# One product on 8 partitions for the relative-bias tables, rows repeated by the DMA; top-k's second tile turned three units later

## What is computed

```python
sc = jnp.einsum('bshpc,hpkc->bshpk', q, sub_keys).astype(jnp.float32)
top_v, top_i = lax.top_k(sc, PEER_TOPK)
...
best_v, best_pos = lax.top_k(cand_v, PEER_TOPK)
idx = jnp.take_along_axis(cand_i, best_pos, axis=-1)
gate = jax.nn.softmax(best_v, axis=-1)
```

```python
dist = qi - kj
in_win = (dist >= 0) & (dist < SWA_WINDOW)
bias = rel_bias.astype(jnp.float32)[t5_bucket(jnp.maximum(dist, 0))]
...
s = jnp.where(valid[None, :, None, None], s + bias[None, None], -jnp.inf)
```

## Time and profile before

| | |
|---|---|
| median of 3 runs | 2253.37 us (2249.6 to 2253.55) |
| the profiled execution | 2255.65 us |
| its span | 2254.1 us |
| TensorE busy (PE) | 2179.7 us, 97% |
| DVE, ScalarE (ACT), GpSimd (POOL) busy | 1362.5, 1228.5, 918.5 us |
| mean DMA rate | 165 GB/s |

### The profile page before, as it was taken

The page is one execution under the profiler, slowest core; times in us unless marked ns, Lnnn a source line. Parts: engine busy times, 40 slices in busy tenths (PEclk is TensorE's granted clock), DMA queues, the critical chain, the costliest instruction groups (busy, mean ns, idle before and its releaser), DMA issues.

```text
span 2254.1 us, 38404 instructions
## 1 busy us (share of the span) xinstructions
PE 2179.7 (97%) x15186; PEld 2037.3 (90%) x15186; DVE 1362.5 (60%) x2552; ACT 1228.5 (55%) x2201; POOL 918.5 (41%) x429
## 2 busy tenths in 40 slices
PE   8999899999999999999999998999999999899999
PEld 7988889999999998888888898999998899799997
DVE  3557652998666756666665765356654764546664
ACT  5657544455777765455453555645445355555443
POOL 4664436898666640000006674450002666361000
PEclk9999999999999999999999999999999999999999
DMA  6544455665444456666664554455665445355664
GB/s 211 157 125 121 148 161 178 181 186 167 141 141 141 148 182 194 195 192 193 195 179 155 190 164 126 123 183 155 184 189 174 150 141 162 109 161 167 182 184 158
DMA packets 104085, 371.70 MB, mean 165 GB/s; under 512 B 11490, under 2 KB 13922, under 8 KB 103268
## 3 DMA queue, kind: packets, MB, share of 16 engines
q1 hardware_dynamic: 103908, 369.25, 53.7%
HBM read 365.53 MB, written 3.67 MB: 164 GB/s over the span
## 4 chain that ended last, share of the span: by engine, by line
PE 78%; DVE 13%; ACT 5%; issue 2%; DMA 1%; POOL 1%; SPq 0%; DVEq 0%; ACTq 0%; POOLq 0%
PE stream_bank L558 13%; PE stream_bank L560 13%; PE stream_bank L559 13%; PE side_bank L560 10%; PE side_bank L558 10%; PE side_bank L559 10%; PE side_bank L811 1%; ACT unit_hi L1071 1%; PE side_bank L810 1%; PE side_bank L620 1%; DVE hot L1942 1%; ACT squares L1097 1%; PE side_bank L639 1%; DVE hot L1945 1%; POOL unit_lo L2326 1%
## 5 line engine op out<-in xcount | busy, mean ns | idle before, releaser
L2326 POOL TENSOR_TENSOR unit_lo<-raw,unit_hi 128x1024 fp32r<-128x1024 f32 (+1 forms) x362 | 880.0, 2436 | 500.3 <-ACT unit_hi L1071 499.0
L1071 ACT ACTIVATE unit_hi<-raw 128x1024 fp32r<-128x1024 f32 (+1 forms) x678 | 708.3, 1045 | 212.5 <-PE side_bank L560 91.4
L1601 DVE TENSOR_TENSOR unit_lo<-raw,unit_hi 128x1024 fp32r<-128x1024 f32 (+1 forms) x316 | 386.4, 1223 | 275.9 <-ACT unit_hi L1071 275.4
L558 PE MATMUL stream_bank<-hT_hi,unit_hi 128*128 128x256 f32 x1672 | 493.3, 295 | 1.0 <-POOL unit_lo L2326 1.0
L559 PE MATMUL stream_bank<-hT_lo,unit_hi 128*128 128x256 f32 x1672 | 477.3, 285 | 0.0
L560 PE MATMUL stream_bank<-hT_hi,unit_lo 128*128 128x256 f32 x1672 | 477.2, 285 | 0.0
L558 PEld LDWEIGHTS stream_bank<-hT_hi,unit_hi 128*128 128x128 f32 x1672 | 325.1, 194 | 9.9 <-issue 6.3
L558 PE MATMUL stream_bank<-h2T_hi,unit_hi 128*128 128x256 f32 x1152 | 330.8, 287 | 0.0
L560 PE MATMUL stream_bank<-h2T_hi,unit_lo 128*128 128x256 f32 x1152 | 327.0, 284 | 0.0
L559 PE MATMUL stream_bank<-h2T_lo,unit_hi 128*128 128x256 f32 x1152 | 326.9, 284 | 0.0
L559 PEld LDWEIGHTS stream_bank<-hT_lo,unit_hi 128*128 128x128 f32 x1672 | 324.9, 194 | 1.6
(11 more groups left out here) (343 smaller groups left out, 4128.5 us busy)
## 6 DMA issues: line engine op xcount, KB each, us to landing
raw<-in_peer_u_dram SPq DMA_DIRECT2D x128, 512.0 KB, 3.6
raw<-in_peer_v_dram SPq DMA_DIRECT2D x128, 512.0 KB, 3.6
raw<-in_gate_dram SPq DMA_DIRECT2D x64, 512.0 KB, 3.6
raw<-in_gt_dram SPq DMA_DIRECT2D x44, 512.0 KB, 3.6
raw<-in_up_dram SPq DMA_DIRECT2D x44, 512.0 KB, 3.6
raw<-in_ffn_out_dram SPq DMA_DIRECT2D x44, 512.0 KB, 3.6
raw<-in_branch_dram SPq DMA_DIRECT2D x32, 512.0 KB, 3.7
raw<-in_w_gate_dram SPq DMA_DIRECT2D x24, 512.0 KB, 3.6
```

The lines of the kernel that those rows point to most:

```text
L558: mm(out, l.hi, r.hi, start=start, stop=False)
L1071: activation(k.unit_hi[n % SPLIT_SLOTS][:, 0:w], k.raw[n % RAW_SLOTS][:, 0:w], ACT.Copy).then_inc(k.sem("unit_hi"), 1)
L1601: V.tensor_tensor(k.unit_lo[s][:, 0:w], k.raw[n % RAW_SLOTS][:, 0:w], k.unit_hi[s][:, 0:w], ALU.subtract).then_inc(unit_lo, 1)
L2326: G.tensor_tensor(k.unit_lo[s][:, 0:w], k.raw[n % RAW_SLOTS][:, 0:w], k.unit_hi[s][:, 0:w], ALU.subtract).then_inc(k.sem("unit_lo_pool"), 1)
```

## The change

Two groups of edits. The second tile's turn goes from behind unit 54 to behind unit 57, its exponential from 46 to 49, the groups of gates start at unit 58 and are spread over 67. And the bias rows are made by one product with the 8 heads on 8 partitions, one addition on 8 partitions; SP writes them 128 times over, by a source that repeats each partition's row with a step of 0, behind the layer's load 11; the wait for the landing and the eight fetches begin at load 16.

```diff
-GATES_FROM, GATES_OVER = 55, 70
-SLOTS_EXP, SLOTS_TURN = (21, 46), (28, 54)
+GATES_FROM, GATES_OVER = 58, 67
+SLOTS_EXP, SLOTS_TURN = (21, 49), (28, 57)
...
-        self.rel_wide = self.place("rel_bias_wide", [P, SWA_HEADS, P], at=at + 8 * SKEW + 32)
-        self.bias_rows = self.place("bias_rows", [P, SWA_HEADS, SKEW], at=at + 8 * SKEW + 32 + 4096)
+        self.bias_rows = self.place("bias_rows", [P, SKEW], at=at + 8 * SKEW + 32)
...
-            for h in range(SWA_HEADS):
-                bank = take(SIDE + 2 + h % 2, ("bias", h))
-                if h == 0:
-                    pe.wait_ge(k.sem("landed_bias_consts"), 32)
-                    pe.wait_ge(k.sem("rel_wide"), 1)
-                mm(bank[:, 0:SKEW], k.rel_wide[0:BUCKETS, h, :], k.bias_consts[0:BUCKETS, 0:SKEW],
-                   start=True, stop=True).then_inc(k.sem("bias_mm"), 1)
-                yield
-            for h in range(SWA_HEADS):
+            bank = take(SIDE + 2, ("bias",))
+            pe.wait_ge(k.sem("landed_bias_consts"), 32)
+            mm(bank[0:SWA_HEADS, 0:SKEW], k.rel_bias[0:BUCKETS, :], k.bias_consts[0:BUCKETS, 0:SKEW],
+               start=True, stop=True).then_inc(k.sem("bias_mm"), 1)
+            yield
+            for _ in range(SWA_HEADS):
                 yield
...
-            for _ in range(5 + 2 * SWA_HEADS):
+            for _ in range(6 + SWA_HEADS):
                 yield
             act.wait_ge(k.sem("landed_bias_rows"), 16)
...
-            dve.wait_ge(k.sem("landed_bias_consts"), 32)
-            V.tensor_copy(k.rel_wide[0:BUCKETS, :, :], wide(k.rel_bias[0:BUCKETS, :], P)).then_inc(k.sem("rel_wide"), 1)
+            dve.wait_ge(k.sem("bias_mm"), 1)
+            V.tensor_tensor(k.bias_rows[0:SWA_HEADS, :], k.bank[SIDE + 2][0:SWA_HEADS, 0:SKEW],
+                            k.bias_consts[0:SWA_HEADS, SKEW:], ALU.add).then_inc(k.free[SIDE + 2], 1)
             yield
...
-    load_until(U["cg.0", 0] + 19)
+    load_until(U["cg.0", 0] + 12)
     scratch = nc.dram_tensor("bias_scratch", [SWA_HEADS * P * SKEW], F32, kind="Internal").ap()
-    sp.wait_ge(*k.over["bias", SWA_HEADS - 2])
-    sp.wait_ge(*k.over["bias", SWA_HEADS - 1])
-    fetch(scratch.rearrange("(h p m) -> p h m", h=SWA_HEADS, p=P), k.bias_rows[:, :, :], "landed_bias_rows")
+    sp.wait_ge(*k.over[("bias",)])
+    rows = k.bias_rows[0:SWA_HEADS, :].unsqueeze(1).to_broadcast([SWA_HEADS, P, SKEW])
+    fetch(scratch.rearrange("(h p m) -> h p m", h=SWA_HEADS, p=P), rows, "landed_bias_rows")
     for h in range(SWA_HEADS):
-        load_until(U["cg.0", 0] + 19 + h)
+        load_until(U["cg.0", 0] + 16 + h)
         if h == 0:
             sp.wait_ge(k.sem("landed_bias_rows"), 16)
```

More of the change, by code:

```diff
@@ L2041, in bias_tables @@
         def bias_tables():
-            for _ in range(4):
+            for _ in range(5):
                 yield
-            dve.wait_ge(k.sem("landed_bias_consts"), 32)
-            V.tensor_copy(k.rel_wide[0:BUCKETS, :, :], wide(k.rel_bias[0:BUCKETS, :], P)).then_inc(k.sem("rel_wide"), 1)
+            dve.wait_ge(k.sem("bias_mm"), 1)
+            V.tensor_tensor(k.bias_rows[0:SWA_HEADS, :], k.bank[SIDE + 2][0:SWA_HEADS, 0:SKEW],
+                            k.bias_consts[0:SWA_HEADS, SKEW:], ALU.add).then_inc(k.free[SIDE + 2], 1)
             yield
[L2047 to L2053, removed]
+            for _ in range(SWA_HEADS):
                 yield
```

## The result

| | us |
|---|---|
| before, median of 4 runs | 2253.46 (2249.6 to 2253.71) |
| after, median of 4 runs | 2267.59 (2263.54 to 2270.52) |
| ratio | 1.0063, 95% interval 1.005 to 1.0076 |
| after, the profiled execution; its span | 2268.49; 2267.0 |

The changed kernel is slower by 0.6%, about 14 us.

A forecast was written before the change was run, and what follows sets the result against it. TensorE, busy 97% of the span, was taken as the bound. Terms -8.2 - 6.9 + 14.8 + 2.6, with 0.2 for the lo half, gave +2.5: 2255.9 us on the median, 8-in-10 range 2236 to 2262.

The forecast's parts named there:

- Term 2: Layer's relative-bias rows: one TensorE product in place of eight gains 6.9 us, the five waits on `bias_rows` included.
- Term 3: Bias write to DRAM from 8 partitions takes 31 us to landing, delays layer unit 12's load: stall 14.8 us, low clock 2.6.
- rival A: Bias write lands within 16.2 us and is hidden, so no stall: 2238.5 us; chance 0.35.
- beyond T = 16.2, one for one: T is the bias write's time from issue to landing; TensorE stalls at layer unit 12 by whatever exceeds 16.2 us.
- The low clock behind the stall: After the stall at layer unit 12 TensorE comes back at the low clock, costing 2.6 us.
- Term 1: Top-k's second turn, unit 54 to 57: gains 8.2 us (5.4 stall, 2.4 low clock, 0.4 turn at low clock).
- rival C: POOL and DVE collide differently, `picked` ends over 3.2 us later, TensorE stalls at unit 57: 2246.5 us; chance 0.02 with write hidden.
- rival B: Same write stall with T over 33 us: 2261.9 us at two engines' worth, 2296.9 at one; chance 0.26.

The follow-up runs named there:

- the 128-partition kernel: Changed kernel with each head's bias column repeated 16 times, so one product fills 128 partitions and the write repeats each row 8 times: 2242.85 us, ratio 0.9959.
- The three narrow widths: Bias rows written from 8 partitions (the changed kernel), 16 or 32 adjacent partitions, otherwise as in the change: 2267.59, 2254.39 and 2242.88 us.
- the 17-us write: Changed kernel with bias rows on 16 partitions, 2254.39 us; with ScalarE evicting units 9 and 10 before unit 12's hi half, 2249.51 us.

## Why the prediction was wrong

**Term 2, one product for eight, -6.9: right.** Six products fewer in the stretch gave 5.95 in the 128-partition kernel (5.9 forecast), the changed kernel's trace has one product left, of 0.81, and no wait on `bias_rows`. With 128 partitions and the turn the kernel is 9.2 us faster, 2.5 of it the turn: 6.7.

**Term 3, the write's time, 31: right, within 1.5 us.** 32.5 by itself, and 34.0 to unit 12's hi half with the load's 1.45 behind it. As far as the rows go this was luck: 31 was the middle of two bounds, three and two engines' worth, and no row set either. The estimate by the Trainium skill's port table, which had 31.1, gave a reason for it and was borne out, and rival A, a write hidden by its cover, fell.

**Term 3, where the stall begins: the step that failed.** I wrote: "Unit 12 began at 1233.72; six of the seven products taken out lie before it, so it now wants to begin at 1233.72 - 5.9 = 1227.8", and from that "beyond T = 16.2, one for one". The data are wanted then, but they are waited for earlier. Every engine that prepares the stream waits for a load three units before TensorE uses it, and has other work queued behind that wait: ScalarE the eviction of unit 9, GpSimd the rotary multiply of unit 9. The stall began at 1214.4, ahead of unit 10, and was 23.3 us where 14.8 was forecast: by the forecast's own rule a write of 32.5 gives 16.3, and the start of the stall two units sooner makes up the rest. The three narrow widths show the true point at 9.1 to 9.8 us, and changing the order alone took 5 us of stall away from the 17-us write. I had even asked, of SP's and ScalarE's wait for `landed_bias_rows`, what stands behind them; I did not ask it of the wait for the delayed load. The low clock behind the stall, 2.6 forecast, came to about 1.9: of the 23.3 the rotary product waits 0.6 in any case, and 24.6 less 22.7 is left. The whole term: 24.6 in place of 17.4.

**Term 1, the turn, -8.2: mis-sized.** Every row behind it was read rightly, and the mechanism is as told, but the 5.4 us of stall and the 2.4 of low clock were one execution's: the step that failed here is taking the price of the turn from one profile. Its time, 2255.65, lay 2.28 above the median, and the forecast only shifted the sum by that. Two further profiles of the same top-k have 3.25 and none, with no low clock. Timed, the term is -2.5 (-0.5 to -4.5). In rows of the changed kernel the turn comes free (no wait on `picked`), and the waits on lo halves are 1.5 us, as in the second profile of before (1.0 in the first), so rival C took no part.

**The sum.** Forecast +2.5; with the two terms as measured, -2.5 - 6.7 + 24.6 = +15.4; measured +14.2. The forecast's rival B, this same mechanism with a longer write, was on the right side but for the wrong reason: it wanted T over 33, where 32.5 was enough with the stall begun ahead of unit 10 and not of unit 12.

## What to carry to other kernels

Ask of a late load not when its data are used, but which instruction first waits for it, on each engine, and what stands behind that instruction; the slack ends there. A write from few adjacent partitions can be slow (32.5 us from 8, 5.7 from 128, for the same bytes), by the ports that they lie behind if the Trainium skill's table (page "SBUF — State Buffer", section "Door 1: The DMA port swizzle") holds as it did in six shapes; and a product can fill all partitions for the price of a few, so repeat rows in the product (16 times here) and let the DMA repeat only the rest. Before pricing a stall on an engine that runs close behind another, look at a second profile; a profiled execution above the median may be above it by just that stall.

## What the runs showed of the hardware that was not expected

- 64 adjacent partitions are no faster a source than 32 (9.36 and 9.40 us for 1536 KB), and 8 partitions 16 apart are nearly twice as fast as 8 adjacent (16.96 and 32.45).
- A transfer with 8 outermost kept the DMA engines busy half as much as one with 16 (0.46 and 0.87) and took as long (16.96 and 17.05 us), both from few partitions (8 that are 16 apart, and 16 adjacent).
- A slow transfer on ScalarE's queue still delayed a load on SP's: it came some 13 us later than with a fast write ahead of it on its own queue.
- A stall of 3.25 us left TensorE's granted clock at 1.00; stalls of 4.1, 5.4, 9.2 and 23.3 us were followed by 0.50, for some 3 to 6 us of the work behind them. The length of the stall alone does not tell: one of 3.3 us in the kernel before (L620 behind DVE's `diag_rms`, ended at 331) was followed by 0.50, in 332 to 335.
- The same kernel's second turn waits 5.41 us or not at all, from one execution to the next.
